# Gates stage of an expert layer: one 256-column product per token, both halves scaled on ScalarE, expert tiles rounded on GpSimd

## What is computed

```
q = (xc @ w_query).reshape(PEER_CHUNK, PEER_HEADS, 2, PEER_HALF)
...
eidx = e1 * PEER_N_KEYS + e2
gate = jax.nn.softmax(top, axis=-1)
act = jax.nn.gelu(jnp.einsum('td,thkd->thk', xc, u).astype(jnp.float32), approximate=False)
wts = (gate * act).astype(xc.dtype)
return jnp.einsum('thk,thkd->td', wts, vv)
```

## Time and profile before

| | us |
|---|---|
| median of 3 runs | 3811.1 (3804.64 to 3813.28) |
| the profiled execution | 3804.55 |
| its span, first to last instruction | 3802.8 |
| TensorE matmul busy | 3611.8 (95%) |
| VectorE busy | 2979.4 (78%) |
| ScalarE busy | 1723.1 (45%) |
| GpSimd busy | 754.4 (20%) |
| first gates stage, from about 930.4 to 1321.6 | 391.2 |
| second gates stage, from about 2876 to 3269 | 393 |

### The profile page before, as it was taken

One profiled execution on the slowest core, in us unless ns is written; L12 is line 12 of the kernel. 1 busy time (PEld: TensorE's weight loads), 2 busy tenths in 40 slices (PEclk: granted clock), 3 DMA queues, 4 the chain that ended last, 5 costly groups with the idle time before them and its releaser, 6 DMA issues. The chain is left out here.

```text
span 3802.8 us, 54896 instructions
## 1 busy us (share of the span) xinstructions
PE 3611.8 (95%) x19550; PEld 3161.4 (83%) x19550; DVE 2979.4 (78%) x6568; ACT 1723.1 (45%) x3281; POOL 754.4 (20%) x523
## 2 busy tenths in 40 slices
PE   8868999999999999999898989899999999999999
PEld 7546788999999988888787657788999999888887
DVE  5674653998988799999686585545998888799998
ACT  4424443334666633333443464342335666433333
POOL 0000000001333245544000000000003333345442
PEclk9989999999999999999998999999999999999999
DMA  4342322455999899999322102223557999899997
GB/s 148 150 157 90 99 67 100 135 167 184 317 307 309 282 392 404 404 404 402 138 90 67 45 1 89 88 82 116 162 167 259 312 313 306 314 401 402 405 404 298
DMA packets 371888, 853.50 MB, mean 224 GB/s; under 512 B 35728, under 2 KB 184848, under 8 KB 368912
## 3 DMA queue, kind: packets, MB, share of 16 engines
q1 hardware_dynamic: 258912, 530.84, 39.9%
q0 software_dynamic: 73728, 268.47, 18.6%
q10 hardware_dynamic: 38976, 50.68, 3.9%
HBM read 753.26 MB, written 95.42 MB: 223 GB/s over the span
## 5 line engine op out<-in xcount | busy, mean ns | idle before, releaser
L1307 POOL DMA_INDIRECT p2f_row<-in_expert_u_rows,p2f_index x128 | 173.2, 1353 | 1331.0 <-POOLq L83 1057.8
L1307 POOL DMA_INDIRECT p1f_row<-in_peer_u_rows,p1f_index x128 | 174.2, 1361 | 965.8 <-POOLq L83 689.9
L1919 PE MATMUL p1v_out<-p1a_u_hi,p1v_w_hi 128*128 128x512 f32 x768 | 298.9, 389 | 0.4 <-DVE p1v_w_lo L1904 0.4
L1919 PE MATMUL p2v_out<-p2a_u_hi,p2v_w_hi 128*128 128x512 f32 x768 | 298.8, 389 | 0.4 <-DVE p2v_w_lo L1904 0.4
L1919 PE MATMUL p2v_out<-p2a_u_hi,p2v_w_lo 128*128 128x512 f32 x768 | 298.8, 389 | 0.0
L1919 PE MATMUL p2v_out<-p2a_u_lo,p2v_w_hi 128*128 128x512 f32 x768 | 298.8, 389 | 0.0
L1919 PE MATMUL p1v_out<-p1a_u_hi,p1v_w_lo 128*128 128x512 f32 x768 | 298.8, 389 | 0.0
L1919 PE MATMUL p1v_out<-p1a_u_lo,p1v_w_hi 128*128 128x512 f32 x768 | 298.8, 389 | 0.0
L1307 POOL DMA_INDIRECT p2f_row<-in_expert_v,p2f_index x128 | 202.1, 1579 | 241.1 <-DVE p2f_sum L1330 220.4
L1307 POOL DMA_INDIRECT p1f_row<-in_peer_v,p1f_index x128 | 199.8, 1561 | 237.8 <-DVE p1f_sum L1330 216.8
L1882 ACT CAST p1a_u_hi<-p1a_u 128x1024 fp32r<-128x1024 f32 x128 | 135.0, 1055 | 159.2 <-PE p1v_out L1919 144.9
(11 more groups left out here) (774 smaller groups left out, 10868.0 us busy)
## 6 DMA issues: line engine op xcount, KB each, us to landing
p1a_u<-in_peer_u SPq DMA_DIRECT2D x128, 512.0 KB
p1a_u<-in_peer_v SPq DMA_DIRECT2D x128, 512.0 KB
p2a_u<-in_expert_u SPq DMA_DIRECT2D x128, 512.0 KB
p2a_u<-in_expert_v SPq DMA_DIRECT2D x128, 512.0 KB
gates<-p_kept SPq DMA_DIRECT2D x20, 2048.0 KB, 12.1
acts<-p1a_a ACTq DMA_DIRECT2D x128, 192.0 KB
p1w_a<-acts SPq DMA_DIRECT2D x128, 192.0 KB
acts<-p2a_a ACTq DMA_DIRECT2D x128, 192.0 KB
```

The lines of the kernel that those rows point to most:

```text
L1307: self.nc.gpsimd.indirect_dma_start(self.row[:, n % self.RING, :], None, self.u_rows if dot else self.v_rows, bass.IndirectOffsetOnAxis(ap ...
L1919: last = nc.tensor.matmul(out[:, o, :], lhs[:, s, t * P:(t + 1) * P], rhs[:, n % VSLABS, cols], start=(n == 0 and m == 0), stop=(n == KEYS ...
```

## The change

VectorE makes both one-hots unscaled, each for four tokens in one instruction. A token's first-key one-hot has two halves side by side (`hot1[r][:, q, 0]` and `[:, q, 1]`); ScalarE writes the second half from the first, scaled by the gate's remainder, and then scales the first in place by the rounded gate: eight instructions a step instead of four. The remainder is the plain difference now, without the reciprocal. TensorE makes one matmul of 256 columns per token and no accumulation; the product buffer holds two steps of two halves instead of four steps. ScalarE copies the first half to `kept` (`top_kept`), and VectorE adds the second (`summed`): the steps of tile i-1 are added behind the one-hots of tile i. `prod_free` comes from the addition. The rounding of the expert tiles in the gates stage (`split_hi`, four tiles ahead) goes from ScalarE to GpSimd, where it stands in front of the fetches of each tile; it waits for the tile's matmuls and for the loaded tile as before. In the choosing stage ScalarE still rounds.

```diff
--- before.py
+++ after.py
@@ -1389,26 +1389,27 @@
         for s in range(self.KEPT):
             sp.wait_ge(self.a_stored[s], 16 * len(range(s, upto, self.KEPT)))
 
-    def split_hi(self, act, n):
+    def split_hi(self, eng, copy, n):
         if n >= KEYS:
             return
         if n >= self.SLABS:
-            act.wait_ge(self.pre_ready, n - self.SLABS + 1)
-        act.wait_ge(self.u_in[n % self.LOADS], 16 * (n // self.LOADS + 1))
-        self.nc.scalar.copy(self.u_hi[:, n % self.SLABS, :], self.u[:, n % self.LOADS, :]).then_inc(self.u_hi_ready, 1)
+            eng.wait_ge(self.pre_ready, n - self.SLABS + 1)
+        eng.wait_ge(self.u_in[n % self.LOADS], 16 * (n // self.LOADS + 1))
+        copy(self.u_hi[:, n % self.SLABS, :], self.u[:, n % self.LOADS, :]).then_inc(self.u_hi_ready, 1)
 
     def split_begin(self, act):
         for n in range(self.SLABS):
-            self.split_hi(act, n)
-
-    def gelu(self, act, n):
+            self.split_hi(act, self.nc.scalar.copy, n)
+
+    def gelu(self, act, n, rounds=True):
 
         act.wait_ge(self.pre_ready, n + 1)
         if n >= self.KEPT:
             act.wait_ge(self.a_stored[n % self.KEPT], 16 * (n // self.KEPT))
         self.nc.scalar.activation(self.a[:, n % self.KEPT, :], self.pre[:, n % 2, 0:DENSE], ACT.Gelu).then_inc(
             self.gelu_done, 1)
-        self.split_hi(act, n + self.SLABS)
+        if rounds:
+            self.split_hi(act, self.nc.scalar.copy, n + self.SLABS)
         self.store(act, n)
 
     def split_lo(self, dve, n):
@@ -1703,14 +1704,16 @@
     base = TT * EARLY
     with ExitStack() as ctx:
         sb, ps, sem = phase_tools(nc, ctx, tag)
-        hot1, hot2 = (sb(n, [P, RING, TOK, KEYS], F32R) for n in ("hot1", "hot2"))
-        hot1_rest = [x[:, TOK * n:TOK * (n + 1), 0:P] for x in (A.x_hi, A.x_lo) for n in range(2)]
-        gate_hi = hot1[:, 0].rearrange("p q k -> p (q k)")[:, 0:DENSE]
+        hot2 = sb("hot2", [P, RING, TOK, KEYS], F32R)
+        own = sb("hot1", [P, 2, TOK, 2, KEYS], F32R)
+        hot1 = [x[:, :, 0:P].rearrange("p (q h) k -> p q h k", h=2) for x in (A.x_hi, A.x_lo)] + [own[:, n] for n in range(2)]
+        gate_hi = own[:, 0].rearrange("p q h k -> p (q h k)")[:, 0:DENSE]
         spare = W.g[:, 1].rearrange("p a g t -> p (a g t)")
-        gate_rest, floor, gate_top = (spare[:, n * DENSE:(n + 1) * DENSE] for n in range(3))
-        prod = ps("prod", [P, RING, TOK, KEYS])
+        gate_rest, gate_top = (spare[:, n * DENSE:(n + 1) * DENSE] for n in range(2))
+        prod = ps("prod", [P, 2, TOK, 2, KEYS])
         A.place(ps)
         hot_ready, hot_free, prod_free = sem("hot_ready"), sem("hot_free"), sem("prod_free")
+        top_kept = sem("top_kept")
         step, top_made, rest_known, rest_ready = (sem(n) for n in ("step", "top_made", "rest_known", "rest_ready"))
         stored = [sem(f"stored{s}") for s in range(KEPT_PIECES)]
         block = ctx.enter_context(nc.Block())
@@ -1725,12 +1728,17 @@
             ch = Chain(dve, step)
             dve.wait_ge(top_made, 1)
             ch.add(V.tensor_copy(gate_top, gate_hi))
-            ch.add(V.tensor_scalar(floor, gate_hi, TINY, None, ALU.max))
-            ch.add(V.tensor_tensor(gate_rest, gate[:], gate_hi, ALU.subtract))
             ch.wait()
-            ch.add(V.reciprocal(floor, floor))
-            ch.wait()
-            V.tensor_tensor(gate_rest, gate_rest, floor, ALU.mult).then_inc(rest_known, 1)
+            V.tensor_tensor(gate_rest, gate[:], gate_hi, ALU.subtract).then_inc(rest_known, 1)
+
+        def summed(dve, t, i):
+
+            for q in steps_after(i):
+                s = t * STEPS + q
+                dve.wait_ge(top_kept, s + 1)
+                part = kept[:, t % KEPT_PIECES, :, q * TOK:(q + 1) * TOK]
+                nc.vector.tensor_tensor(part, prod[:, s % 2, :, 1, :].rearrange("p q k -> p k q"), part,
+                                        ALU.add).then_inc(prod_free, 1)
 
         @block.vector
         def _(dve):
@@ -1743,21 +1751,27 @@
                         r = s % RING
                         if s >= RING:
                             dve.wait_ge(hot_free, s - RING + 1)
-                        for q in range(TOK):
-                            token = s * TOK + q
-                            nc.vector.tensor_scalar(hot1[:, r, q, :], C["iota"][:, 0:KEYS], first[:, token:token + 1],
-                                                    gate_top[:, token:token + 1], ALU.is_equal, ALU.mult)
-                        nc.vector.tensor_tensor(
-                            hot2[:, r], C["iota"][:, 0:KEYS].unsqueeze(1).broadcast_to([P, TOK, KEYS]),
-                            second[:, s * TOK:(s + 1) * TOK].unsqueeze(2).broadcast_to([P, TOK, KEYS]),
-                            ALU.is_equal).then_inc(hot_ready, 1)
+                        for hot, keys in ((hot1[r][:, :, 0, :], first), (hot2[:, r], second)):
+                            last = nc.vector.tensor_tensor(
+                                hot, C["iota"][:, 0:KEYS].unsqueeze(1).broadcast_to([P, TOK, KEYS]),
+                                keys[:, s * TOK:(s + 1) * TOK].unsqueeze(2).broadcast_to([P, TOK, KEYS]), ALU.is_equal)
+                        last.then_inc(hot_ready, 1)
+                    if i > 0:
+                        summed(dve, t, i - 1)
+                    elif t > 0:
+                        summed(dve, t - 1, LATE - 1)
                     for n in fetch.steps(t * LATE + i):
                         fetch.take(dve, n)
+            summed(dve, PIECES - 1, LATE - 1)
 
         @block.gpsimd
         def _(pool):
-            for n in range(FETCHED_IN_GATES + fetch.RING):
+            for n in range(fetch.RING):
                 fetch.fetch(pool, n)
+            for i in range(KEYS - base):
+                A.split_hi(pool, nc.gpsimd.tensor_copy, base + i + A.SLABS)
+                for n in fetch.steps(i):
+                    fetch.fetch(pool, n + fetch.RING)
 
         @block.tensor
         def _(pe):
@@ -1768,12 +1782,11 @@
                         r = s % RING
                         pe.wait_ge(hot_ready, s + 1)
                         pe.wait_ge(rest_ready, s + 1)
-                        if s >= RING:
-                            pe.wait_ge(prod_free, s - RING + 1)
+                        if s >= 2:
+                            pe.wait_ge(prod_free, s - 1)
                         for q in range(TOK):
-                            for m, hot in enumerate((hot1[:, r], hot1_rest[r])):
-                                last = nc.tensor.matmul(prod[:, r, q, :], hot2[:, r, q, :], hot[:, q, :],
-                                                        start=(m == 0), stop=(m == 1), skip_group_check=True)
+                            last = nc.tensor.matmul(prod[:, s % 2, q], hot2[:, r, q, :], hot1[r][:, q],
+                                                    start=True, stop=True, skip_group_check=True)
                         last.then_inc(hot_free, 1)
 
         def rest_of_hot(act, s):
@@ -1782,7 +1795,8 @@
             act.wait_ge(hot_ready, s + 1)
             for q in range(TOK):
                 token = s * TOK + q
-                last = nc.scalar.mul(hot1_rest[r][:, q, :], hot1[:, r, q, :], gate_rest[:, token:token + 1])
+                nc.scalar.mul(hot1[r][:, q, 1, :], hot1[r][:, q, 0, :], gate_rest[:, token:token + 1])
+                last = nc.scalar.mul(hot1[r][:, q, 0, :], hot1[r][:, q, 0, :], gate_top[:, token:token + 1])
             last.then_inc(rest_ready, 1)
 
         @block.scalar
@@ -1793,15 +1807,14 @@
                 for i in range(LATE):
                     for q in steps_after(i):
                         rest_of_hot(act, t * STEPS + q)
-                    A.gelu(act, base + t * LATE + i)
+                    A.gelu(act, base + t * LATE + i, rounds=False)
                     for q in steps_after(i):
                         s = t * STEPS + q
-                        r = s % RING
                         if q == 0 and t >= KEPT_PIECES:
                             act.wait_ge(stored[t % KEPT_PIECES], 16 * (t // KEPT_PIECES))
                         act.wait_ge(hot_free, s + 1)
                         nc.scalar.copy(kept[:, t % KEPT_PIECES, :, q * TOK:(q + 1) * TOK],
-                                       prod[:, r].rearrange("p q k -> p k q")).then_inc(prod_free, 1)
+                                       prod[:, s % 2, :, 0, :].rearrange("p q k -> p k q")).then_inc(top_kept, 1)
                     for g in fetch.groups(t * LATE + i):
                         fetch.gelu(act, g)
 
```

## The result

The changed kernel takes 3888.9 us (median of 4 runs, 3884.17 to 3890.08) against 3810.2 for the kernel before beside it (4 runs, 3804.64 to 3813.28): a ratio of 1.0206, 95% interval 1.0193 to 1.0218. Predicted were 3890 us in a range of 3798 to 3965, and the sign slower. The profiled execution took 3890.08 us, its span 3888.3.

The account below looks back on a forecast made before the run. TensorE bounds the gates stages now at 32.2 us a piece; after the change VectorE would, 29.3 us plus roundings making 35.5. That is 3.3 more, +79 us in 24 pieces, added to the median 3811.1: 3890 us, range 3798 to 3965.

Parts of the forecast that it names:

- TensorE's part: Gates stages: four 256-column products at 0.12 us replace eight of 128; a piece takes 29.2 us, 3.0 us less.
- The DMA rival: Gates stages: DMA, busy 0.91, becomes the bound; 0.95 in a 30.8 us piece, could take a few us; no separate chance.
- ScalarE's part: Gates stages: loses rounding, gains scalings, +3.8 us a piece with over 9 spare; TensorE waits 0.8 us twice a piece.
- VectorE's own work: Gates stages: subtractions, unscaled one-hots, additions and fetched rows take 29.3 us a piece without collisions.
- GpSimd's part, which decides: Gates stages: 68 roundings a stage, 1.1 us each, and VectorE's two-SBUF-input instructions exclude each other; chance 0.68.
- 35.5 us a piece: VectorE's piece in the gates stages if roundings exclude it: 29.3 + 68/12 x 1.1, longer than TensorE's 30.8.
- the fill's slope: GpSimd fill at 0.83 ns an element; by its slope and start a 1024-element rounding takes 0.97 us; 1.1 was taken.
- the contrast with the kernel before: Gates stages: new VectorE instructions but the addition have two SBUF inputs; before, four of five in a one-hot step did not.
- VectorE never idles: Gates stages: VectorE sets the pace and is busy nearly throughout, so its 35.5 us sum is the piece.
- At the end of the stage: nothing together: Gates stage ends: one more addition, +0.7 us, against the reciprocal chain gone in front, -0.6 us: nothing together.
- sharing without harm: Rival: GpSimd's roundings don't hold up VectorE in the gates stages; piece 30.8 us, -34 us, 3777 us; chance 0.14.
- The roundings under the additions: Rival: roundings run beside VectorE's additions, hiding 0.61 us each; piece 32.0 us, 3807 us; chance 0.10, half or wholly hidden.

Follow-up runs that it names:

- the experiment with the product alone: Kernel before with one 256-column product per token in place of two of 128, second half's sum left out, so no addition: 3774.8 us, ratio 0.9911.
- the fills: Changed kernel with each GpSimd rounding in the gates stages replaced by a fill of the same 1024 elements that reads nothing: 3809.2 us, ratio 1.0004.
- the four versions here that were forecast from the engines' sums: Three product buffers, addition two tiles late: rounding on ScalarE 3839.7 us; three of six roundings on GpSimd 3808.3; two 3803.1; two, ScalarE scaling one step further ahead 3802.6.
- the version with three product buffers: Changed kernel with three product buffers, addition two tiles late, rounding on ScalarE after copies and scalings, rows six tiles earlier: 3839.7 us, ratio 1.0087.

## Why the prediction came out, step by step

- *TensorE's part* held. Four products take 0.64 or 0.71 us of record, 0.12 apart. Of the 72 us that 3.0 us a piece make in 24 pieces, the experiment with the product alone shows 33 in the time. The DMA rival took part in it: there, tiles were late at a stage of 375 us, with a share of 0.93.
- *ScalarE's part*: the two waits a piece came as foreseen, 24 in a stage, but last 1.6 us and not 0.8. Of that, 1.2 us is there with the fills too, where nothing collides: behind Gelu and the issue of its store, the copy starts 0.6 us after the stream of products and not 0.2. The rest comes from VectorE's late one-hots, for which ScalarE waits 35 us a stage (5 with the fills). That ScalarE has room to spare was right only with the rounding gone from it.
- *VectorE's own work* held: 29.3 us a piece, 352 a stage, against 350.1 where nothing collides. The addition at 0.69 held.
- *GpSimd's part, which decides*, held as mechanism: one after the other, in both directions. Its size was wrong. The mis-sized term was the one in "35.5 us a piece", with the full 1.1 us of each of 68 roundings, 75 us a stage, on VectorE; the runs show 46.7. A rounding alone takes 1.04 us, and the VectorE instruction behind it is typically 0.84 us longer (1.53 for 0.68); where VectorE idles when it starts (6 of 68) it costs at most 0.19. The 1.04 us also settle the length: the fill's slope was near, and the 1.44 and 1.54 us that the prediction considered are out. And the contrast with the kernel before was wrong: its scaled one-hots are held up as well.
- *VectorE never idles* was wrong. The prediction took the piece for VectorE's sum. It waits 18.5 us a stage for the copy that its addition needs. 352 + 46.7 + 18.5 = 417 of the 420.2 us. Too much for the roundings and too little for the waits made 35.5 us a piece where 35.0 was measured.
- *At the end of the stage: nothing together* was the step that failed. It counted the addition and the reciprocal chain, and not GpSimd, whose fetches are asked for by VectorE and whose drain ended 8.5 us after the last of them in the kernel before too. It had 0.7 us of cover left before; with VectorE in step with TensorE the cover is gone: +9.6 and +10.0 us, a quarter of the loss.
- *TensorE's clock* was not in the sum: 1.00 before, 0.96 in the stage after, for up to 10 us in all.
- *The rivals*: sharing without harm is out (the stage with fills shows what it would have been: 3809, and not 3777, since the 24 waits of 1.2 us between steps and the hole eat the gain). The roundings under the additions needed a wait to get there, and then gave 23.5 us, not the 84 that hiding 0.6 us in each would have; fewer than half started in one.

So the near hit, 3890 for 3888.9, is luck in its size: the terms left out or mis-sized are -28 (roundings), +19 (VectorE's wait) and +10 us (the hole) a stage, and nearly cancel. The sign and the mechanism were foreseen. What the change loses is the GpSimd read: 36 of 39 us per stage. Without it the rest of the change is worth 6.6 us in the stage and loses 9.8 in the hole.

## What to carry to other kernels

Before an elementwise pass moves to GpSimd, count VectorE's instructions beside it that can't run with it, and the idle time that VectorE has to lose. Instructions with both inputs in SBUF are of this kind, and so were the scaled one-hots with one; a meeting typically costs VectorE 0.84 us, 0.69 us on average over all roundings, for a pass of 1.04. Fills on GpSimd, and additions out of PSUM on VectorE, passed freely. When an engine loses its lead over the one that sets the pace, look at everything that the lead had hidden, above all at what ends the stage. And an engine's sum is a lower bound of a piece, not the piece: the four versions here that were forecast from the engines' sums had a longer first gates stage, one by over 20 us, the others by 2 to 14.

## What the runs showed of the hardware that was not expected

- GpSimd's closing drain ended 7.8 to 12.5 us after its last instruction where that was a fetch and 6.9 to 7.0 where it was a rounding, over both gates stages of all the traces here. Where nothing covered it, it held the next stage for 10 to 12.4 us.
- TensorE's granted clock fell from 1.00 to 0.50 seven times in a stage, each time at a wait of 1.6 to 1.7 us, with 2 to 5 us of slow matmuls behind it, and rose again under full work. Such waits also came without a fall: 13 in the same stage, and 22 in the version with three product buffers. Eight matmuls of no use in each wait between a tile's steps kept it up but for one fall.
- A rounding on GpSimd took 1.04 us alone and up to 4.4 us in a row of two-input instructions of VectorE.
- Scaled one-hots of VectorE, with one tensor from SBUF and no operand in PSUM, took up to 1.79 us beside roundings and at most 0.58 without.
